# Streamed operand tiles of a float32r matrix product moved from a multiple of 64 bytes to 16 and 48 bytes behind one

## What is computed

```python
# first block, per layer
x = x + jnp.concatenate([y_mix, y_mem], axis=-1) @ w_out[layer]
x = x + sqrelu_mlp(rms_norm(x, norm_mlp[layer]), w_mlp_in[layer], w_mlp_out[layer])
# second block, per layer
p = h @ w_in[l]
x = x + gt1 * (mixed @ w_out[l])
gate, up = jnp.split(h2 @ w_gu[l], 2, axis=-1)
x = x + gt2 * ((jax.nn.silu(gate) * up) @ w_down[l])
```

## Time and profile before

| | |
|---|---|
| median of 3 executions | 2758.15 us (2756.61 to 2761.39) |
| profiled execution, its own time | 2760.57 us |
| its span, first to last instruction | 2758.8 us |
| TensorE busy, products | 2714.3 us, 98% |
| TensorE weight loads | 2257.0 us, 82% |
| VectorE / ScalarE / GpSimd busy | 57% / 36% / 7% |
| mean granted TensorE clock | 0.996 |
| the three lines of `three`, share of the chain that ended last | 25% each |

### The profile page before, as it was taken

The page is one execution under the profiler, slowest core; times in us unless marked ns, Lnnn a source line. Parts: engine busy times, 40 slices in busy tenths (PEclk is TensorE's granted clock), DMA queues, the critical chain, the costliest instruction groups (busy, mean ns, idle before and its releaser), DMA issues.

```text
span 2758.8 us, 45685 instructions
## 1 busy us (share of the span) xinstructions
PE 2714.3 (98%) x19372; PEld 2257.0 (82%) x19372; DVE 1585.8 (57%) x2330; ACT 990.7 (36%) x1373; POOL 187.5 (7%) x272
## 2 busy tenths in 40 slices
PE   9999999999999999999999999999999999999999
PEld 7888888898688888877878888888878778888887
DVE  6758777764577777665453543334584454633334
ACT  5642222344532222353333332223553333422223
POOL 4000000000000000001050000000010220000000
PEclk9999999999999999999999999999999999999999
DMA  5334555521045555320032232232220123232231
GB/s 161 114 114 152 176 161 176 160 77 62 17 135 175 177 169 162 104 86 19 3 97 92 94 105 92 95 104 81 77 66 10 33 92 107 77 107 92 96 99 65
DMA packets 239934, 281.19 MB, mean 102 GB/s; under 512 B 9718, under 2 KB 227330, under 8 KB 239746
## 3 DMA queue, kind: packets, MB, share of 16 engines
q1 hardware_dynamic: 226426, 226.29, 25.7%
q0 software_dynamic: 13184, 52.11, 6.4%
q10 hardware_dynamic: 136, 0.03, 0.0%
HBM read 276.31 MB, written 2.10 MB: 101 GB/s over the span
## 4 chain that ended last, share of the span: by engine, by line
PE 91%; DVE 4%; ACT 2%; issue 2%; POOL 1%; DMA 0%; DVEq 0%; SPq 0%; ACTq 0%; POOLq 0%
PE psum L2617 25%; PE psum L2618 25%; PE psum L2619 25%; DVE wlo L1691 1%; PE psum L2698 1%; PE psum L2699 1%; PE psum L2700 1%; PE psum L3229 1%; PE psum L3214 1%; PE psum L3197 1%; PE psum L2632 1%; PE psum L3253 1%; POOL mo L887 1%; ACT whi L948 0%; PE psum L3186 0%
## 5 line engine op out<-in xcount | busy, mean ns | idle before, releaser
L2617 PE MATMUL psum<-hh,whi 128*128 128x512 f32 (+1 forms) x2016 | 781.5, 388 | 4.8 <-DVE wlo L1691 4.4
L2618 PE MATMUL psum<-hl,whi 128*128 128x512 f32 (+1 forms) x2016 | 772.2, 383 | 0.3 <-issue 0.3
L2619 PE MATMUL psum<-hh,wlo 128*128 128x512 f32 (+1 forms) x2016 | 772.0, 383 | 0.0
L1691 DVE TENSOR_TENSOR wlo<-raw,whi 128x2048 fp32r<-128x2048 f32 x217 | 499.4, 2302 | 449.5 <-ACT whi L948 449.0
L948 ACT ACTIVATE whi<-raw 128x2048 fp32r<-128x2048 f32 x217 | 414.4, 1910 | 523.8 <-PE psum L2619 519.2
L2617 PE MATMUL psum<-mh,whi 128*128 128x512 f32 (+1 forms) x1248 | 485.4, 389 | 0.3 <-DVE wlo L1691 0.3
L2618 PE MATMUL psum<-ml,whi 128*128 128x512 f32 (+1 forms) x1248 | 479.1, 384 | 0.0
L2619 PE MATMUL psum<-mh,wlo 128*128 128x512 f32 (+1 forms) x1248 | 479.0, 384 | 0.0
L2617 PEld LDWEIGHTS psum<-hh,whi 128*128 128x128 f32 x2016 | 379.3, 188 | 92.0 <-issue 8.7
L2619 PEld LDWEIGHTS psum<-hh,wlo 128*128 128x128 f32 x2016 | 379.3, 188 | 74.5
L2618 PEld LDWEIGHTS psum<-hl,whi 128*128 128x128 f32 x2016 | 379.6, 188 | 72.7 <-issue 0.9
(11 more groups left out here) (487 smaller groups left out, 2781.4 us busy)
## 6 DMA issues: line engine op xcount, KB each, us to landing
rest<-in_ada_w POOLq DMA_DIRECT2D x64, 768.0 KB, 5.3
raw<-in_w_gu SPq DMA_DIRECT2D x44, 1024.0 KB, 5.1
raw<-in_w_in SPq DMA_DIRECT2D x34, 1024.0 KB, 5.2
raw<-in_w_mlp_in SPq DMA_DIRECT2D x32, 1024.0 KB, 5.4
raw<-in_w_mlp_out SPq DMA_DIRECT2D x32, 1024.0 KB, 5.1
raw<-in_w_out SPq DMA_DIRECT2D x16, 1024.0 KB, 5.1
raw<-in_w_down SPq DMA_DIRECT2D x16, 1024.0 KB, 4.9
raw<-in_w_mem_kv SPq DMA_DIRECT2D x8, 1024.0 KB, 5.3
```

The source lines that it names most:

```text
L1691: ins = dve.tensor_tensor(wlo[:, g % 2, :, :], raw[:, g % 2, :, :], f32(whi[:, g % 2, :, :]), ALU.subtract)
L2617: pe.matmul(out, whi_, xhi, start=first, stop=False)
L2618: pe.matmul(out, whi_, xlo, start=False, stop=False)
L2619: return pe.matmul(out, wlo_, xhi, start=False, stop=last)
```

## The change

hh and hl are now two views into one buffer `h_parts` that has 4 elements (16 bytes) more at each end, and mh and ml two views into `m_parts`. ho and mo are views that begin at the same places. `padding` has 32 bytes in place of 160. By the built program h_parts begins at 98048 (a multiple of 64) and m_parts at 130848 (32 behind one). So hh and hl begin 16 bytes behind a multiple of 64, mh and ml 48 behind one, and `rest` begins at 163648, a multiple of 64. whi, wlo and raw are where they were. No instruction is added, removed or moved on any engine; in the profile the four tiles are called h_parts and m_parts, and line numbers from there on are higher by one.

```diff
-        sb("padding", [P, 40])
+        sb("padding", [P, 8])
 
         e = ExitStack()
-        hh = sb("hh", [P, KT, T], F32R, e)
-        hl = sb("hl", [P, KT, T], F32R, e)
+        AT, HALF = 4, KT * T
+        parts = sb("h_parts", [P, 2 * HALF + 2 * AT], F32R, e)
+        hh, hl = (parts[:, AT + i * HALF:AT + (i + 1) * HALF].rearrange("p (k n) -> p k n", k=KT) for i in range(2))
         e.close()
-        ho = sb("ho", [P, 2 * KT * T])
+        ho = sb("ho", [P, 2 * HALF + 2 * AT])[:, AT:AT + 2 * HALF]
 
         e = ExitStack()
-        mh = sb("mh", [P, KT, T], F32R, e)
-        ml = sb("ml", [P, KT, T], F32R, e)
+        parts = sb("m_parts", [P, 2 * HALF + 2 * AT], F32R, e)
+        mh, ml = (parts[:, AT + i * HALF:AT + (i + 1) * HALF].rearrange("p (k n) -> p k n", k=KT) for i in range(2))
         e.close()
-        mo = sb("mo", [P, 2 * KT * T])
+        mo = sb("mo", [P, 2 * HALF + 2 * AT])[:, AT:AT + 2 * HALF]
```

## The result

| | before | after |
|---|---|---|
| median | 2758.05 us (2756.61 to 2761.39, 4 runs) | **2813.69 us** (2813.14 to 2815.47, 4 runs) |
| ratio, 95% interval | | 1.0201 (1.0183 to 1.0219) |
| profiled execution, its own time / span | 2760.57 / 2758.8 us | 2813.25 / 2811.5 us |

What follows compares the result with a forecast made beforehand. The prediction took TensorE's start-to-start time per product as the bound; 0 + 0 - 17.6 us on 2760.6 gave 2743.0, and 2740.6 us as median, 0.6% faster. Forecast range 2709 to 2752, all runs 2655 to 2795.

Steps and rivals of the forecast that it cites:

- What bounds the kernel: TensorE's products: the time from one start to the next, 226.7 ns for 512 columns, 13.3 ns above the columns.
- Part 1: VectorE and ScalarE working on the shifted tiles: cost 0, with slack in the window of the up products.
- Part 2: DMAs of x tiles, mem and output on shifted places in mo: 0, at most +9 us.
- Part 3: Streamed operand of the three products of `three`: 1.8 ns saved on each of 9792 products, -17.6 us.
- the wide slab: Nearest row for the price: 96 products of 264 columns, 121.5 ns apart, extra 11.5 ns against 13.3 on aligned products.
- The rival of the worse pattern: Linear products' stream settles in a worse pattern: up to 5.8 ns each, +57 us, 2815; chance 0.27 with ragged end.
- start-up rows: Four intervals after a stream's start, 32.88 to 33.81 us, averaging 232.5 ns before falling to 226.7; extra 19.2 ns.
- ragged end: Smaller form of the slower rival: one more 32-byte read per product, 3.3 ns, +32 us, 2791; chance 0.27 with worse pattern.
- Full relief: Rival for the streamed products: the 13.3 ns extra goes almost wholly, -101 us, 2657; chance 0.16.
- No difference: Rival: start places do nothing, as for plain fp32 products; 2758 us, chance 0.26.
- sum line: Adds the three parts, 0 + 0 - 17.7 = -17.6 us, on the profiled execution's 2760.6 us: 2743.0.
- six plain fp32 rows: Upper end of a gain: six plain fp32 products taken as 430 ns apart, about 3 ns above their columns.

Runs made afterwards that it cites:

- experiment 9: Kernel before with the weights and both pairs of tiles moved together by 64 bytes, distance kept: 2758.38 us, ratio 1.0001.
- experiment 10: Kernel before with only the weights moved up by 128 bytes and the padding cut as much, hh and mh left to the byte: 2804.38 us, ratio 1.0170.
- experiment 11: Kernel before with weights and tiles moved together by 32 bytes, distance kept: 2759.52 us, ratio 1.0003.
- experiment 1: Small kernel of float32r products only, starts of stream and weights and column count varied; stream shifted by 0 bytes 233 ns, by 4 239, by 64 227.
- experiment 4: Changed kernel with hh and hl 32 bytes behind a multiple of 64, mh and ml on one: 2817.64 us, ratio 1.0221.
- experiment 6: Kernel before with padding cut from 40 to 24 elements, both pairs of tiles moved together by 64 bytes: 2807.57 us, ratio 1.0184.
- experiment 7: Kernel before with padding cut from 40 to 8 elements, both pairs of tiles moved together by 128 bytes: 2804.56 us, ratio 1.0173.
- four small kernels: Kernels with nothing but float32r products, each with its own weight load, mapping starts of stream and weights in various steps; floor about 226.6 ns with 512 columns.
- experiment 3: Changed kernel with whi 16 and wlo 48 bytes behind a multiple of 64 as well: 2774.46 us, ratio 1.0061.
- experiment 5: Small kernel of products only, stream and weights at 8 x 8 places in steps of 16 bytes, two passes; 226.7 ns at (0, 0).
- experiment 12: Kernel before with only wlo moved, by 32 bytes, padding cut by as much, tiles and whi left to the byte: 2812.97 us, ratio 1.0197.

## Why the prediction was wrong

- **What bounds the kernel: right.** The time from start to start decides, and the loss is there and nowhere else (+55.8 us on the long products, -3.2 on the short ones, +52.7 in the span). Of the 9792 products in the sum, though, only the 9216 of 512 columns paid; the 576 of 256 columns took 0.6 us less together.
- **Part 1, VectorE and ScalarE at 0: right.** 750 ns for the same group, and idle time before line 2618 of 3.3 us.
- **Part 2, DMAs at 0 to +9: right, near 0.** Landing of x went from 5.5 to 6.0 us, the output's stayed at 3.7. Even the 0.5 us can't be put down to alignment: experiments 9, 10 and 11, whose tiles begin at multiples of 32, had 5.9, 6.1 and 5.8. And the first 512-column product of `three` began at 25.3 us, against 26.1 before.
- **Part 3, the streamed operand at -1.8 ns: this step failed, in sign and size.** It had the extra fall from 13.3 to 11.5 ns; it rose to 20. Measured against the -1.8: +6.7 ns where the stream is settled, +6.3 over all. Its price came from the wide slab, as the row nearest in type, rate and weight loads. But the wide slab isn't near in what mattered. Its products stream 264 columns of the *weight slab* past a block of the tile, and moving that block changed 121.5 ns into 121.4. In experiment 1, 264 columns took 120.0 ns with the stream shifted by 0, 16 or 32 bytes alike. So the lower extra of this length isn't owed to the odd starts, and it said nothing about where a 512-column stream goes.
- **The premise under it: wrong.** The prediction counted places modulo 64 and asked what leaving the aligned place does, with 13.3 ns as the normal price of an aligned product and room below. Experiment 1 has aligned starts at 233 ns, experiments 4, 6 and 7 aligned tiles at 232 to 234 in the kernel itself. 13.3 was the *best* case, held by a coincidence that the views of one product can't show: weights and all streamed tiles at 128 by 256 (experiments 6, 7 and 10 end it with a shift by 64 or 128 bytes, 9 and 11 keep it). Their addresses stood in the text on the kernel: 98176 - 49792 and 130944 - 66432 are both multiples of 256. The question a reader should have put is which relations between operands hold now and are broken, not only which alignment.
- **The rival of the worse pattern: right in kind, and near in size, in part by luck.** It had +5.8 ns and 2815 us from the start-up rows; measured +6.7 and 2813.7. The stream does settle in a steady slower rhythm. That the time fits so closely is luck: a price too low was put on 576 products too many. And no run shows that the rhythm behind a break and the settled one are the same thing. Its chance, with the ragged end, was 0.27, but its argument against ("they die out after a few products") took for general what held for one placement: with other addresses the same 233 ns stay for good. And the range stopped at 2795, short of this rival's own time, although a row of the trace had the number.
- **Full relief (2657): nothing in it.** No place in four small kernels went below 226.6 ns with 512 columns. The Trainium skill (TensorE: Matmul & The Clock Gate, Back-to-back issue gap) has 215.8 ns for 512 columns, which it gives for an isolated product. For float32r products with a weight load each, the settled groups here measured 226.6 to 240.
- **No difference (2758): refuted.** Plain fp32 stayed indifferent: at least 379 ns per record in line 2730 from either place, before and after. float32r isn't. The Trainium skill (SBUF — State Buffer, Specifications) with its lines of 16 bytes would give 0 for the change's starts at 16 and 48, and for experiment 7's shift by 128; measured were 56 and 47 us.
- **Two slips that moved nothing.** The sum line writes -17.7 where its term is -17.6. And the six plain fp32 rows at 430 ns are records, of which such a product leaves two: one product takes 860 ns.

**What stays open.** What the 13.3 ns are that even the best place pays, and which part of SBUF or of the read path makes the distance modulo 256 count. That it is two reads, of stream and weights, that meet is suggested by the distance being what counts; no run shows it directly. Nor is there a formula for the price: experiment 3's 229 ns (mean) stand at places that no map covers, and how much of the change's loss its starts off a multiple of 32 add to that of the broken distance was not separated. Moving the second pair alone was not tried. Nor did a version beat the kernel before: its placement is at the floor of all maps.

## What to carry to other kernels

When a kernel is one long stream of products, a shift of a large buffer can change its speed, even by a whole 128 bytes and even of a padding: write down the addresses of all operands that meet in a product, and look at their differences modulo 256, and at whether they are multiples of 32, before calling an edit of the layout neutral. For float32r products of 512 columns with a weight load each, starts at multiples of 32 and equal modulo 256 kept 226.7 ns (226.6 to 227.4 over all maps); most other placements cost 1 to 3% more per product, the worst 6%, and of the others that reached 226.7 only some repeated it. And take a price from a neighbouring row only after asking in which regime the row is: columns and roles of the operands are part of it, not only data type and clock.

## What the hardware did that was not expected

- What a product costs depends on how the addresses of its stream and its weights relate. The stream alone by 32 bytes: 233.3; both by 32: 226.7; the stream alone by 256: 226.6.
- The good placement of one length is not that of another. At a distance of 192, where 512 columns take 233, 256 columns take 113.3, less than the 120.0 of the kernel's own 256-column products at a distance of 0; and the change, bad for 512 columns, took those from 120.0 to 118.1.
- Some places have two rhythms. The weights alone at 12 or 16 bytes gave 230.0 and 233.4 in one pass, 226.7 and 226.7 in the other; only what ran before and the PSUM bank differed. In experiment 5 one place with the same bank in both passes changed in the same way (226.7 and 233.4), so what ran before can decide alone.
- One operand in three out of place costs as much as all (700 ns per triple in experiment 12 and in the changed kernel).
